# Branch stage of a hybrid trunk: which weights are loaded early, and all of them multiplied in two fp32r parts

## The reference

```
z = h @ w_in                       # 53 output tiles; the last three are "Z"
o_a = attention(...); o_b = gmlp(...); o_c = rmsnorm(deltanet(...)) * silu(zc)
g_a, g_b, g_c = sigmoid(gates)
merged = g_a*(o_a @ wb[0]) + g_b*(o_b @ wb[1]) + g_c*(o_c @ wb[2])   # wb[i]: 512 x 1024
x = x + gate1 * rmsnorm(merged @ w_out)                              # w_out: 1024 x 1024
h2 = rmsnorm(x) * (1 + scale2) + shift2                              # then the FFN or the experts
mod = silu(c) @ ada_w + ada_b      # adaLN: shift, scale, gate of each sub-layer
```

## Time and profile before

| | |
|---|---|
| median of 3 runs | 1819.18 us (1812.81 to 1821.51) |
| profiled execution | 1815.65 us, span 1813.5 us, mean granted TensorE clock 0.995 |
| busy | PE 1755.4 us (97%), DVE 1020.1 (56%), ACT 790.3 (44%), POOL 257.7 (14%) |
| chain that ended last | PE 81%, DMA 6%, DVE 5%, ACT 4%, issue 2%, POOL 1% |

### The profile page before, as it was taken

How to read it: one execution, slowest core, us unless ns; L and a number is a source line. 1 busy time by engine, 2 the same in 40 slices (tenths; PEclk the granted TensorE clock), 3 DMA queues, 4 the chain that set the end, 5 groups by cost and what they waited for, 6 DMA issues and landing times.

```text
span 1813.5 us, 32205 instructions
## 1 busy us (share of the span) xinstructions
PE 1755.4 (97%) x13983; PEld 1462.4 (81%) x13983; DVE 1020.1 (56%) x1379; ACT 790.3 (44%) x1108; POOL 257.7 (14%) x228
## 2 busy tenths in 40 slices
PE   5999999999999999999999999999999999999997
PEld 4889788987979999888898788887978555556885
DVE  2866645444745344326965545545748544345887
ACT  3355732234335233225366523235356433335775
POOL 2620033241000000003500223330002000000001
PEclk9999999999999999999999999999999999999999
DMA  9661152216453434337541323127567988979994
GB/s 359 202 246 59 52 218 71 95 48 231 142 208 105 139 100 132 139 132 284 189 171 53 124 100 118 48 89 237 216 222 259 364 307 319 343 276 389 385 379 197
DMA packets 175189, 351.27 MB, mean 194 GB/s; under 512 B 5161, under 2 KB 60481, under 8 KB 174544
## 3 DMA queue, kind: packets, MB, share of 16 engines
q1 hardware_dynamic: 170880, 334.50, 51.8%
q0 software_dynamic: 4176, 14.82, 2.3%
HBM read 320.46 MB, written 28.84 MB: 193 GB/s over the span
## 4 chain that ended last, share of the span: by engine, by line
PE 81%; DMA 6%; DVE 5%; ACT 4%; issue 2%; POOL 1%; SPq 0%; POOLq 0%; DVEq 0%; ACTq 0%
PE bank L1806 6%; PE bank L1195 6%; PE bank L1197 5%; PE bank L1196 5%; PE bank L1666 3%; PE bank L1668 3%; PE bank L1782 3%; PE bank L1667 3%; PE bank L1235 3%; PE bank L1783 3%; PE bank L1785 3%; PE bank L1237 3%; PE bank L1236 3%; PE bank L1614 2%; PE bank L1119 2%
## 5 line engine op out<-in xcount | busy, mean ns | idle before, releaser
L1965 ACT ACTIVATE ring_split<-ring 128x1024 fp32r<-128x1024 f32 (+2 forms) x84 | 119.2, 1447 | 178.2 <-DMA ring<-in_ffn_w_up 101.8
L1197 PE MATMUL bank<-hT_hi,ring_split 128*128 128x384 f32 x576 | 193.4, 336 | 0.0
L2884 DVE TENSOR_TENSOR ring_split<-ring,ring_split 128x2048 fp32r<-128x2048 f32 (+1 forms) x28 | 73.8, 2670 | 141.5 <-ACT ring_split L1965 141.5
L1195 PE MATMUL bank<-hT_hi,ring_split 128*128 128x384 f32 x384 | 139.8, 364 | 0.7 <-DVE modv L2540 0.5
L1237 PE MATMUL bank<-ring_split,hT_hi 128*128 128x256 f32 x480 | 135.2, 282 | 0.0
L793 DVE TENSOR_TENSOR ring_split<-ring,w_upper_a 128x2048 fp32r<-128x2048 f32 (+2 forms) x54 | 96.4, 1814 | 59.2 <-PE bank L1806 39.4
L1196 PE MATMUL bank<-hT_lo,ring_split 128*128 128x384 f32 x384 | 128.4, 334 | 0.0
L1666 PE MATMUL bank<-hT_hi,ring_split 128*128 128x384 f32 x352 | 119.1, 338 | 0.0
L1668 PE MATMUL bank<-hT_hi,ring_split 128*128 128x384 f32 x352 | 118.6, 337 | 0.0
L1667 PE MATMUL bank<-hT_lo,ring_split 128*128 128x384 f32 x352 | 117.2, 333 | 0.0
L1235 PE MATMUL bank<-w_gran,hT_hi 128*128 128x256 f32 x384 | 107.7, 280 | 1.3 <-ACT ktok L1965 1.3
(11 more groups left out here) (464 smaller groups left out, 4338.4 us busy)
## 6 DMA issues: line engine op xcount, KB each, us to landing
ring<-in_w_in SPq DMA_DIRECT2D x28, 2048.0 KB, 9.3
ring<-in_ada_w SPq DMA_DIRECT2D x24, 2048.0 KB, 8.8
ring<-in_moe_w_down SPq DMA_DIRECT2D x18, 1536.0 KB, 7.7
ring<-in_moe_w_gate SPq DMA_DIRECT2D x26, 1024.0 KB, 6.0
ring<-in_moe_w_up SPq DMA_DIRECT2D x26, 1024.0 KB, 8.7
ring<-in_w_branch SPq DMA_DIRECT2D x8, 1536.0 KB, 11.5
ring<-in_ffn_w_gate SPq DMA_DIRECT2D x11, 1024.0 KB, 5.3
ring<-in_ffn_w_up SPq DMA_DIRECT2D x11, 1024.0 KB, 7.9
```

What stands on the lines that cost most here:

```text
L1195: mm(out, hi, hT_hi[:, k], start=k == 0, stop=False)
L1197: last = mm(out, lo, hT_hi[:, k], start=False, stop=k == KT - 1)
L1965: return go(out, in_, ACT.Copy)
```

## The change

Units 14 and 15 move ahead of the "oc" adaLN units in the ring, the "wo" set is taken apart (its first unit stands ahead of 17, and is issued behind 17 and 18; its second, in layer 0, ahead of 19). The inputs of branches a and b are split during Z, unit 14 too, in halves of 128 columns into the new `w14_hi`; all units are now multiplied in parts. TensorE runs branch groups (0,0), transposes, (0,1), (1,0), (1,1), (0,2), (1,2), then the "oc" units, then m = 2 to 7 with the turn of "oc" after m = 3 and the first "wo" unit after m = 5. The turn of "wo" moves behind the first token tile of the output projection, the warming products here go, and the merged tiles 6 and 7 are waited for one by one. ScalarE's and VectorE's lists follow one common order, `SPLIT`. Helpers that only move are left out below.

```diff
...
@@ -329,8 +329,9 @@
          v3(upper("wo_hi_c", "oT", 0, KT * 512)[:, :], KT))
-O_UP = ("o0", "o1", "o2", "w15", "me0", "w16", "me1", "me2", "w17", "me3", "me4", "w18a", "me5", "me6", "me7", "w18b", "w19a", "w19b")
-O_LO = ("w15", "o0", "o1", "o2", "me0", "w16", "me1", "me2", "w17", "me3", "me4", "w18a", "me5", "me6", "me7", "w18b", "w19a", "w19b")
+w14_hi = upper("w14_hi", "conv", 1536, 12 * 256)[:, :].rearrange("p (m q n) -> p m q n", m=2, q=12)
+SPLIT = ("o0", "o1", "w14a", "w14b", "w15", "o2", "me0", "me1", "w16", "me2", "me3", "w17", "me4", "me5", "w18a", "w18b", "me6", "me7",
+         "w19a", "w19b")
 WO_K = dict(w18a=(18, 0, 6), w18b=(18, 6, 8), w19a=(19, 0, 4), w19b=(19, 4, 8))
@@ -554,14 +555,20 @@
 FF_GU, FF_DN = 11, 6
 order = [("ada", n) for n in ADA_FIRST]
 for layer, at in enumerate(ADA_AT):
-    for ada, first, last in (("", 0, 2), (0, 2, 3), (1, 3, 4), (2, 4, 7), ("d0", 7, 9), ("d1", 9, 14), ("oc", 14, 18), ("wo", 18, 20), ("nb", 0, 0)):
-        order += [("ada", n) for n in (at["p"][ada:ada + 1] if ada in (0, 1, 2) else at[ada] if ada else ())]
+    for ada, first, last in (("", 0, 2), (0, 2, 3), (1, 3, 4), (2, 4, 7), ("d0", 7, 9), ("d1", 9, 14), ("", 14, 16), ("oc", 16, 17),
+                              ("wo0", 17, 19), ("wo1", 19, 20), ("nb", 0, 0)):
+        order += [("ada", n) for n in (at["p"][ada:ada + 1] if ada in (0, 1, 2) else at["wo"][int(ada[2]):int(ada[2]) + 1] if ada in ("wo0", "wo1")
+                                 else at[ada] if ada else ())]
         order += [(kind, layer, i) for i in range(first, last) for kind in (("w", "w_hi") if 7 <= i < 14 else ("w",))]
     if layer == 0:
         order += [(kind, i) for i in range(FF_GU + FF_DN) for kind in ("ff", "ff_hi")][:-1]
     order += [("ada", n) for n in at["n4"]]
 U_MOE = len(order)
+issue = list(range(U_MOE))
+for at in ADA_AT:
+    u = order.index(("ada", at["wo"][0]))
+    issue[u:u + 3] = [u + 1, u + 2, u]
 M_GU, M_DN, M_SLOT = 6, 4, 5
...
@@ -654,6 +661,11 @@
         eng.wait_ge(down_mm, at[0] - FF_GU + 1)
     else:
         wait(eng, "y_mm", 0, 2 * NT)
+def branch_done(m, b):
+    first = ((0, 0), (0, 1), (1, 0), (1, 1), (0, 2), (1, 2))
+    return first.index((m, b)) + 1 if m < 2 else 3 * m + b + 1
 def ff_rows(u):
...
@@ -823,7 +835,8 @@
     sp.dma_start(cst[:, :], cst_d[:, 0:NRES]).then_inc(cst_in, 16)
     sp.dma_start(xt[:, 0], x_prompt[0]).then_inc(x_in, 16)
     sp.dma_start(xt[:, 1:3], x_sample[0].rearrange("(t p) n -> p t n", p=P)).then_inc(x_in, 16)
-    for u, (kind, *at) in enumerate(order):
+    for u in issue:
+        kind, *at = order[u]
         if u == 1:
             sp.wait_ge(rows_in, 96)
         if kind == "w" and at[1] == 4:
...
@@ -1584,51 +1597,55 @@
         wait(pe, "proj_ev", layer, T_Z)
         token_tiles(layer, T_Z, 13)
-        ada_quads(at["oc"], 6)
+        def branch(m, b):
+            i, cs = 14 + m // 2, slice((m % 2) * P, (m % 2 + 1) * P)
+            low, out = raw_unit(layer, i, True), B[2 + 3 * (m % 2) + b][:, 0:TOK]
+            for k in range(4):
+                q = 4 * b + k
+                high = w14_hi[:, m, q] if i == 14 else wb_hi[(i - 15) % 2][:, q, cs]
+                mm(out, high, o_hi[:, q], start=k == 0, stop=False)
+                mm(out, high, o_lo[:, q], start=False, stop=False)
+                last = mm(out, low[:, q, cs], o_hi[:, q], start=False, stop=k == 3)
+            last.then_inc(S["br_mm"], 1)
+        def lowered(name):
+            wait(pe, "o_lo", layer, SPLIT.index(name) + 1)
+        lowered("w14a")
+        branch(0, 0)
         for t in range(NT):
             wait(pe, "oc_v", layer, t + 2)
             for h in range(DNH):
-                last = tr(B[2 + t][:, h * P:(h + 1) * P], osum[:, t, h * P:(h + 1) * P])
+                last = tr(B[(0, 1, 7)[t]][:, h * P:(h + 1) * P], osum[:, t, h * P:(h + 1) * P])
             last.then_inc(S["oc_mm"], 1)
-        ada_turn(at["oc"], 6, KK_)
-        wait(pe, "oc_ev", layer, 3)
-        for m in range(8):
-            if m == 1:
-                pe.wait_ge(ada_cp, set_end(at["oc"]))
+        branch(0, 1)
+        lowered("w14b")
+        branch(1, 0)
+        branch(1, 1)
+        lowered("o2")
+        branch(0, 2)
+        branch(1, 2)
+        ada_quads(at["oc"], 1)
+        for m in range(2, 8):
             if m % 2 == 0:
-                arrived(unit(14 + m // 2))
-            if m >= 2:
-                wait(pe, "br_ev", layer, m - 1)
-            i, cs = 14 + m // 2, slice((m % 2) * P, (m % 2 + 1) * P)
-            raw, low = raw_unit(layer, i), raw_unit(layer, i, True)
+                lowered(f"w{14 + m // 2}")
+            wait(pe, "br_ev", layer, m - 1)
             for b in range(3):
-                out = B[2 + 3 * (m % 2) + b][:, 0:TOK]
-                if m % 2 == 0 and m and b == 0:
-                    wait(pe, "o_lo", layer, O_LO.index(f"w{i}") + 1)
-                if m == 2:
-                    wait(pe, "o_lo", layer, O_LO.index(f"o{b}") + 1)
-                for k in range(4):
-                    q = 4 * b + k
-                    if i == 14:
-                        last = mm(out, raw[:, q, cs], oT[:, b, k], start=k == 0, stop=k == 3)
-                    else:
-                        high = wb_hi[(i - 15) % 2]
-                        mm(out, high[:, q, cs], o_hi[:, q], start=k == 0, stop=False)
-                        mm(out, high[:, q, cs], o_lo[:, q], start=False, stop=False)
-                        last = mm(out, low[:, q, cs], o_hi[:, q], start=False, stop=k == 3)
-                last.then_inc(S["br_mm"], 1)
-        ada_quads(at["wo"], 0)
-        if layer == 0:
-            keep_warm(1, 4)
+                branch(m, b)
+            if m == 3:
+                ada_turn(at["oc"], 1, ada_buf)
+            if m == 5:
+                for half in range(2):
+                    ada_quad(at["wo"][0], half, 0)
+        for n in at["wo"][1:]:
+            for half in range(2):
+                ada_quad(n, half, 0)
         pe.wait_ge(mod_ok, 4 * layer + 2)
         wait(pe, "br_ev", layer, 7)
         for half in range(2):
             gain_row(layer, 2, 0, half, 2 + half)
-        if layer == 0:
-            keep_warm(1, 10)
-        ada_turn(at["wo"], 0, ada_buf)
-        wait(pe, "o_lo", layer, O_LO.index("me7") + 1)
         for t in range(NT):
             if t == NT - 1:
                 pe.wait_ge(ada_cp, set_end(at["wo"]))
@@ -1638,8 +1655,10 @@
                     if i != 18 + half:
                         continue
                     if t == 0:
-                        wait(pe, "o_lo", layer, O_LO.index(name) + 1)
+                        lowered(name)
                     for k in range(k0, k1):
+                        if t == 0 and half == 0 and k >= 6:
+                            lowered(f"me{k}")
                         high = wo_upper(name)[:, k - k0]
                         mm(out, merged_hi[:, k, ts], high, start=k == 0, stop=False)
                         mm(out, merged_lo[:, k, ts], high, start=False, stop=False)
@@ -1649,6 +1668,7 @@
                 elif t == NT - 1:
                     last.then_inc(S["wo_mm"], 1)
             if t == 0:
+                ada_turn(at["wo"], 0, ada_buf)
                 for half in range(2):
                     wait(pe, "gr_ev", layer, half + 1)
                     gain_row(layer, 2, 1, half, 2 + half)
...
@@ -2218,65 +2238,74 @@
                 copy(D_KWs[:, :, :, CH[half]], kw_bank(half)).then_inc(S["d_uwe"], 1)
             for spot in ("uw", "ws0", "so0", "ws1"):
                 gates_of(pair, spot)
+        g4 = GT[:, :].rearrange("p (b m n) -> p b m n", b=3, m=KT)
...
+        def split_branch(b):
+            copy(o_hi[:, 4 * b:4 * b + 4], oT[:, b]).then_inc(S["o_up"], 1)
+        wait(act, "s_z", layer, 6)
+        split_branch(0)
         wait(act, "s_or", layer, 6)
         go(RX[:, 0:1536], OT[:, 3072:4608], ACT.Square).then_inc(S["oc_sq"], 1)
         wait(act, "oc_v", layer, 1)
         go(oss, oss, ACT.Sqrt, bias=eps1, scale=1.0 / DK).then_inc(S["oc_sq"], 1)
+        split_branch(1)
+        act.wait_ge(s_slot[slot(at_ring("w", layer, 14))], full(at_ring("w", layer, 14)))
+        for m in range(2):
+            copy(w14_hi[:, m], raw_unit(layer, 14)[:, :, P * m:P * (m + 1)]).then_inc(S["o_up"], 1)
+        wait(act, "proj_ev", layer, T_Z)
+        sigmoids(0)
         for t in range(NT):
             evac(T_Z + t, zs[:, t], ACT.Silu)
-        ada_copy(at["oc"], 6, KK_)
+        split_unit(15)
         for t in range(NT):
             wait(act, "oc_mm", layer, 3)
-            copy(oT[:, 2, :, t * P:(t + 1) * P], v3(B[2 + t][:, :], 4)).then_inc(S["oc_ev"], 1)
-        wait(act, "proj_ev", layer, T_Z)
-        g4 = GT[:, :].rearrange("p (b m n) -> p b m n", b=3, m=KT)
...
-        sigmoids(0)
+            copy(oT[:, 2, :, t * P:(t + 1) * P], v3(B[(0, 1, 7)[t]][:, :], 4)).then_inc(S["oc_ev"], 1)
         wait(act, "oc_ev", layer, 3)
-        for b in range(3):
```

(85 more changed lines are left out.)

18 lines of the change are left out of this document (17 added, 1 removed).

## The result

The changed kernel takes 1803.78 us, median of 6 runs (1799.95 to 1805.91), beside 1817.88 us for the kernel before in the same session (6 runs, 1812.41 to 1821.51). The ratio is 0.9934, 95% interval 0.9917 to 0.9952. The forecast was 1803.0. The profiled execution took 1805.91 us, span 1804.0, mean granted clock 0.993.

A forecast was written before the change was run, and what follows sets the result against it. TensorE was taken as the bound. Gains of 11.1 us (layer 0) and 4.15 (layer 1), less 0.7, made 14.6, turning 1815.65 into 1801 and 1819.18 into 1804.6; forecast 1803, between, range 1795 to 1813.

The forecast's parts named there:

- First stretch: End of Z to the last branch product: 58.4 us per layer if nothing waits, gaining 4.7 in layer 0, 3.8 in layer 1.
- Splits in Z: During Z, ScalarE gets 10.2 us more work on 5.55 busy, ending about 2.7 us before Z does.
- the fourth rival: Splits in Z run late and units 14 and 15 wait, 3 us a layer: gain 5 or less, 1813; chance 0.06.
- Unit 16: Branch stage: its load lands in 6.9 us, leaving 1.5 us slack before m=4; later landings pass to TensorE one for one.
- Second stretch: Last branch product to output projection: 3.85 us in layer 0, gain 7.35; 2.3 us in layer 1, gain 2.3.
- Output projection: Turn of the wo units moves in, 0.95 us a layer; unit 19's late first half adds 1.0 in layer 1.
- The rival that it still falls in the stage: Branch stage: one clock fall a layer costs 1.7 us, gain 11.2, 1807; two give 1810; chance 0.14.
- the 3.4 us that I had put on that rule: Branch stage: if transposes read as idle to the clock, the summed gain would be some 3.4 us smaller.
- Ring at the end of layer 0: Projection's end to FFN: first FFN load stands behind the second nb adaLN load, costing 0.7 us; bounds 0 and 3.
- the third rival: End of layer 0: late adaLN and FFN loads make TensorE wait 8 us more, gain 6.6, 1811; chance 0.08.
- the wait of ScalarE "of under 1 us": Sign at layer 0's end: first FFN load issued behind an adaLN load, ScalarE waiting under 1 us for it.
- The sum: Whole kernel: layer 0 gains 11.1, layer 1 4.15, less 0.7 for layer 0's end: 14.6 us.

The follow-up runs named there:

- e3: The changed kernel with unit 16's load held back until the first group of unit 15 is done; 1815.11 us, ratio to before 1.0011.
- e4: The changed kernel with layer 0's unit 18 loaded only when the last group of unit 16 is done; 1806.72 us, ratio to before 0.9972.
- e7: The kernel before without the 14 warming products of layer 0's second stretch; 1816.14 us, ratio to before 1.0012.
- e6: The kernel before with 8 (layer 0) and 4 (layer 1) warming products while TensorE waits for unit 14; 1813.01 us, ratio 0.9999.
- e5: The kernel before with only layer 0's second nb adaLN load held back as the changed kernel holds it; 1818.33 us, ratio 1.0025.
- e2: The changed kernel with the first FFN unit loaded ahead of the second nb adaLN unit; 1798.90 us, ratio to before 0.9922.

## Why the prediction was right, and where it was off

**First stretch.** Forecast 58.4 in both layers, 14.1 of it for unit 14 and the transposes; measured 58.40, 58.32 and 14.01. TensorE had work in every us of it, which is why counting products was enough. How much of the stretch's gain is unit 14 in parts and how much is its earlier load no run separates; the windows give 17.0 us of raw products against 14.01 with the transposes, and 2.25 us of waiting against none.

**Splits in Z** (the fourth rival, "It doesn't do what it says"). The last Z copy on ScalarE starts at 436.60, 0.2 us behind Z's last product, and had waited 1.59 us for TensorE and not the other way round. Z is 17.06 us. ScalarE's 13.58 us fit in; I had counted 10.2 us on top of 5.55.

**Unit 16.** Forecast landed in 6.9 us with 1.5 us of slack. It was issued at 450.46 and ScalarE took it at 457.14, 6.7 us later. VectorE's last step of merge(2) ended at 465.9 and TensorE reached m = 4 at 467.43: slack 1.5. e3 shows that the price of passing it is close to one for one (4.00 and 4.20 us of waiting for 4.5 too late), plus the clock.

**Second stretch.** Forecast 3.85 and 2.3, measured 3.70 and 1.70. e4 brings the merges' dependence on unit 18's landing back. Removing the warming products cost nothing, as forecast, but for a reason that e7 sharpens: it is the waits of 1.43 and 2.73 us that they covered, and the change had removed these.

**Output projection.** Forecast +0.95 and +1.95; measured 35.2 to 36.1 in layer 0 and 35.2 to 37.0 in layer 1, with 0.62 of wait where I took 1.0 for the late half of unit 19.

**The clock.** The rival that it still falls in the stage did not come: 1.00 in all rows of it. The Trainium skill (TensorE: Matmul & The Clock Gate, "Part 4: PE-mode transpose") says that transposes do not count as TensorE activity as products do. The transposes at 438.48, which stand between two product groups, have 1.00 in their window (fourth row above) and behind them, so the 3.4 us that I had put on that rule were not taken. In e6 the transposes before the raw products stayed and the idle time went, and the clock held. What the rule says of a transpose by itself no run here tests. My size for the clock in the kernel before was right for layer 0's raw products (e6: 15.2 us against 17.0), of which 1.1 reached the end of the stage, and right for layer 1 only in the one execution that I had read. Without that fall layer 1's gain is 99.9 - 96.7 = 3.2 instead of 5.1. In time e6 shows neither. On record is also the mean granted clock of every execution: on average 0.9950 and 0.9946 for the kernel before (23 and 29 runs), 0.9948 and 0.9944 for the changed one (6 and 5 runs). Over the whole program the changed kernel stands no less at half clock than before; as far as these means tell, what the stage won in clock was lost elsewhere, in the tail among others.

**Ring at the end of layer 0: the term that was mis-sized.** I took 0.7 us, upper bound 3; it cost 4.2: 2.6 of idle time, and 1.6 of clock behind it, which stood in no term. The order was foreseen: the adaLN load ahead of the first FFN load, ScalarE waiting for that, the rows' copies queued behind it. What I costed was "The FFN gate half adds 1 MB". That half landed 5.5 us behind the projection (529.47 and 10.6), where I had 4.9 (though 2.2 + 2.4 is 4.6). But the wait before the split of the gate half counts both halves of the unit, and the up half, another 1 MB, landed last. Four MB were asked for from 529.06 on and the last arrived at 543.1. ScalarE was ready 4.03 us earlier, at 539.11, just where I had put it (4.5 us after the projection against my 4.4). TensorE then waited 3.31 us for ScalarE's copies, and the clock fell behind that wait, for another 1.6. e5 makes this cost alone (4.3 in the tail, 4.6 in time) and e2 removes it alone (5.0 in the tail, 6.5 in time). The adaLN unit's own wait was 0.64 where I had 0.35. So the third rival, that the end of layer 0 gives it back (chance 0.08), came about at half its size and through the unit's second half, not through another transfer; and one of my signs failed, the wait of ScalarE "of under 1 us", which was 4.03.

**The sum.** Against the profile of before: 11.5 in layer 0's stage, 5.1 in layer 1's, less 4.2 is 12.4, forecast 11.1 + 4.15 - 0.7 = 14.6. With e5's profile for the old stage, which has the fall in layer 0 and none in layer 1, the gains are 108.6 - 97.8 = 10.8 and 99.9 - 96.7 = 3.2, less 4.2 that is 9.8. The median fell by 14.1 in one session and 7.8 in the other; beside the 23 and 29 later runs of before, 1813.17 and 1813.69, the first session's 1803.78 would be a fall of 9.4 to 9.9. The forecast time came out within 1 us, but that is luck in part. The tail was 3.5 us too little and the gain elsewhere 1.4 us too small. The gain of 14.6 is some 5 us more than the later runs of before bear out, and the forecast of 1803 started from one execution of before at 1815.65 and a median of three at 1819.18, which lie 2 to 6 us above the medians of those runs.

## What to carry to other kernels

When a load is moved past another in a shared queue, follow what the waiting engine's semaphore really counts: here a split of one half waited for both, and what had been costed as one MB behind two was two MB behind two. Look for the cost where the ring turns next and not only in the stage that is edited: the stage gained what was counted, and a quarter of it was given back 36 us later, where swapping two list entries recovers it. And before a fall of the clock in one profile is entered as a gain, look for it in a second execution, and run the kernel before often enough: here its median of 6 runs lay 4 to 5 us above that of 23 and 29.

## What the runs showed of the hardware

Half-clock stretches come and go between executions of the same code. The kernel before had one in layer 1's raw products in one profile and none in two others that are the same there. In code that no experiment touched, the ten profiles show one at about 1000 us in all ten (3.4 us long in seven, 6.8 in three), at about 1660 in nine, at about 200 in six and at about 850 in five. From the first FFN product of layer 0 to Z of layer 1 they take from 661.4 to 665.5 us. A change of 1 to 4 us is therefore seen in the windows and hardly in the median of a few runs. All five falls at 850 are in profiles of the changed kernel and its variants (five of six), none in those of the kernel before and its variants (none of four); so few profiles can't tell chance from a side effect of the change, which would cost under 2 us.

A wait can cost more than itself. Of the 4.2 us that the tail lost, 2.6 were idle and 1.6 were the products behind it at 1.2 GHz; in e3, 4.00 us of waiting made 5.6. In e4 no fall followed, and 2.67 + 0.90 us of waiting made 3.8.
